# Storing scattered gate weights for 32 tokens at a time instead of 16, in a two-layer diffusion backbone step

## The chip, the cores and the metric

One core of one Trainium2 chip runs the whole program. The metric is device time in microseconds (us) of one execution; for several executions the median is given. A time of the kernel here is 3,980 us or so, so a tenth of a per cent is about 4 us.

## What is computed

Two trunk layers work on 128 context tokens and 512 latent tokens, 640 in all, 1024 features wide. Layer 0 mixes tokens by retention and a DFT, layer 1 by a convolution module. Each layer ends in the same channel mixer (PEER), and the change lies in that one alone:

```python
def peer(h, w_q, sub_keys, u_tab, v_tab):
    q = (x @ w_q).reshape(T, PEER_HEADS, 2, PEER_DQH)
    scores = jnp.einsum('thsd,hskd->thsk', q, sub_keys)
    s, i = lax.top_k(scores, PEER_TOPK)
    ...
    top, sel = lax.top_k(cand, PEER_TOPK)
    idx = jnp.take_along_axis(cidx, sel, axis=-1)
    g = jax.nn.softmax(top, axis=-1)
    ...
        a = jax.nn.gelu(jnp.einsum('td,thkd->thk', xb, u_tab[ib]))
        w = gb * a
        return jnp.einsum('thk,thkd->td', w, v_tab[ib])
```

Each token picks 8 x 16 = 128 of 16,384 experts. An expert is one row of `u_tab` and one row of `v_tab`; the token's output is the sum of its experts' v rows, each weighted by its gate `g` times the GELU of the token's product with the u row. All numbers are 32-bit floats.

## The kernel before

**Two ways through PEER.** Of the five blocks of 128 tokens, two (`GB = 2`) are done sparsely: GpSimd gathers each token's u and v rows by index (L711, 512 KB a gather), VectorE takes the products (`dot`, L1524) and adds the weighted v rows (`add`, L1559). The other three blocks (`DT` = 384 tokens) are done densely: TensorE multiplies with all 16,384 experts. For 32 of those tokens (`GQ`) the u side is done by gathers too (`qdot`, L1534).

**The dense way has two stages per layer.** In the *jobs* stage (`job`, L807) TensorE computes all u products of 352 tokens, 128 experts at a time, 128 such jobs (and 16 query projections), from weights that SyncE's queue loads into four slots (L591). ScalarE applies the GELU into `a_stage`, and SyncE stores it to DRAM (`acts`, L584) every fourth job. In the *values* stage (`values`, L876) TensorE walks over 32 chunks (`CHUNKS`) of 4 x 128 experts: for a chunk VectorE multiplies the activations read back (`acts`, L620) with the gates read back (L615) into `w_slot` (`weigh`, L1587 to L1601), and 48 matmuls (as the trace counts them) multiply `w_slot` with the chunk's v rows (`v_slot`, loaded at L607 and L623).

**The gates have to be scattered in between.** The dense way needs, for each token, the gates as a 128 x 128 table of experts with 128 entries filled. VectorE and ScalarE build one-hot rows for four tokens at a time (`OH = 4`: `hot`, L1562, L1571 and L1573; `build`, L1145), TensorE multiplies them into a PSUM bank (`scatter`, L844), and ScalarE copies the bank to a staging buffer (`take_scatter`, L1163). These 96 scatters per layer run amid the last two fifths of the jobs stage, placed by a planner's times (`peer_steps_of`, L486), with `LATE = 6`: all scatters stand before the last six jobs. This stretch is called the *scatter stretch* below.

**Staging, store and load.** There are two staging buffers (`g_stage`, L254). Each holds [128 first indices] x [128 second indices x `TQ` tokens]. After the fourth scatter into a buffer ScalarE's queue stores it to DRAM as one 1 MB piece (L1173), 24 a layer. A buffer is written again only after its store has landed (semaphores `g_out`, L1168). In the values stage SyncE loads the gates of two chunks at a time (1.5 MB, L615): 24 pieces per partition, each 8 second indices x 16 tokens x 4 bytes = 512 bytes.

**The queue of SyncE at the handover.** SyncE issues in program order. When the last u weights are issued, `peer_values` (L599) begins: the first chunk's v rows (2 MB, into `work[:, 5120:9216]`) wait for the scores (L603), done long before; then it waits until all scatters are copied and all stores landed (L609 to L611); then come the first gate load (L615), the second chunk's v rows, and the rest. VectorE's first `weigh` waits for that gate load, and TensorE's first values pass for that `weigh` (L888).

```python
1165  q, at = spot(b, g) // 4, g % 4
1167  if at == 0 and q >= 2:
1168      act.wait_ge(g_out[q % 2], l * G_OUT + 16 * (q // 2))
1171  if at == 3:
1172      act.wait_ge(sc_taken, l * len(sc_at[0]) + i + 1)
```

Of the kernel before, what the change touches and what calls it, by code (L numbers as in the profile page):

```python
# [32 lines left out]
NKEYS = 128  # L33
# [5 lines left out]
CT = 4  # L39
CHUNKS = NKEYS // CT  # L40
GCT = 8
TQ = 16
QS = DT // TQ
CE = CT * DT
GE = GCT * DT
# [1 line left out]
KEPT = 2  # L47
OH = 4
OHS = P // OH
HK = PHEADS * TOPK  # L50
GH = GB * PHEADS
ROWS = GH * TOPK
# [9 lines left out]
GQG = GQ // OH  # L62
BUILT = DB * OHS - GQG
LAG = 20
# [82 lines left out]
def program(nc, x_in, cond_t, norm_gain, final_gain, ada_w, ada_b, ada_fix_in, ab_w_in, ab_w_out, decays, states,  # L147
# [3 lines left out]
    with ctx:  # L151
# [10 lines left out]
        work = sb("work", [P, 15872])  # L162
# [88 lines left out]
        load_slot = [ring[:, i * 2048:(i + 1) * 2048] for i in range(4)]  # L251
        u_rows = [ring[:, 8192 + i * D:8192 + (i + 1) * D] for i in range(RING)]
        v_rows = [ring[:, 12288 + i * D:12288 + (i + 1) * D] for i in range(RING)]
        g_stage = [work[:, 10240 + i * 2048:12288 + i * 2048].rearrange("p (j t) -> p j t", j=NKEYS) for i in range(2)]  # L254
        a_stage = [work[:, 2048 + i * CA:2048 + (i + 1) * CA] for i in range(2)]
        hq = hT[:, :, 0:P]
        idx_q = q_t[:, 0:NQ].bitcast(U32)
# [97 lines left out]
        A_OUT, G_OUT, G_IN, A_IN = (16 * n for n in ((CHUNKS - KEPT) // 2, QS // 2, CHUNKS // 4, (CHUNKS - KEPT) // 2))  # L355
# [86 lines left out]
        def dve_order():  # L442
# [9 lines left out]
            picks += shared(NG - 1)  # L452
            hots = [("hot", b, g, 0, 1.45) for b in ORDER for g in range(OHS)]
            for m, hot in enumerate(hots):
# [31 lines left out]
        def peer_steps_of(jobs):  # L486

            ready, clock, begun, choosing = [], BEGIN, [0.0] * SCORE_LEAD, True
            for kind, a, b, i, w in dve_order():
# [18 lines left out]
                if kind == "hot":  # L508
                    ahead = ORDER.index(a) * OHS + b + OHB - 2
                    if ahead < DB * OHS and not 0 <= ahead - (DB - 1) * OHS < GQG:  # L510
                        ready.append((clock + 3, "build", ORDER[ahead // OHS], ahead % OHS))
# [31 lines left out]
        def spot(b, g):  # L543
            return ORDER.index(b) * OHS + g

# [23 lines left out]
        def _(sp):  # L569
# [29 lines left out]
            def peer_values(l):  # L599

                for n, c in enumerate(v_order):
                    if n == 0:
                        sp.wait_ge(scores, (l + 1) * BLOCKS * PHEADS)  # L603
                    elif n < 3:
                        sp.wait_ge(jobs_done, l * len(plans[0][1]) + len(plans[l][1]) - (2 - n) * CT)
                    if n < 3:
# [5 lines left out]
                    if n % 2 == 0:  # L612
                        if n >= 4:
                            sp.wait_ge(w_ready, l * CHUNKS + n - 2)
                        sp.dma_start(g_slot[n // 2 % 2].rearrange("p (q e) -> p q e", q=QS),  # L615
                                     gates_d[l].rearrange("q i e -> i q e")[:, :, c // 2 * GCT * TQ:(c // 2 + 1) * GCT * TQ]).then_inc(g_in[n // 2 % 2], 16)
                    if n >= KEPT:
# [444 lines left out]
        def _(act):  # L1062
# [49 lines left out]
            def peer(l):  # L1112
# [49 lines left out]

                def take_scatter(b, g):  # L1163
                    i = sc_at[l]["scatter", b, g]
                    q, at = spot(b, g) // 4, g % 4
                    act.wait_ge(sc_done, l * len(sc_at[0]) + i + 1)
                    if at == 0 and q >= 2:
                        act.wait_ge(g_out[q % 2], l * G_OUT + 16 * (q // 2))  # L1168
                    f(g_stage[q % 2][:, :, at * OH:(at + 1) * OH],
                      bank[:, 4 + i % SCB, :].rearrange("p (t j) -> p j t", t=OH)).then_inc(sc_taken, 1)  # L1170
                    if at == 3:
                        act.wait_ge(sc_taken, l * len(sc_at[0]) + i + 1)
                        nc.scalar.dma_start(gates_d[l, b * OHS // 4 + g // 4], g_stage[q % 2].rearrange("p j t -> p (j t)"))\  # L1173
                            .then_inc(g_out[q % 2], 16)

                for kind, a, i in steps:
# [27 lines left out]
            for i in range(len(items) + 1):  # L1204
                if i < len(items):
                    c, b = items[i]
# [8 lines left out]
                if 0 <= i - 1 < 4 * BLOCKS:  # L1215
                    c, b = items[i - 1]
# [41 lines left out]
            for i in range(PE_TILES):  # L1258
                t = KT - PE_TILES + i
# [4 lines left out]
            for i in range(PE_TILES):  # L1264
                t = KT - PE_TILES + i
# [27 lines left out]
        def _(v):  # L1293
# [101 lines left out]
            def peer(l):  # L1395
# [191 lines left out]
                def weigh(n):  # L1587
# [6 lines left out]
                    if n >= 3:  # L1594
                        v.wait_ge(v_done, l * (CHUNKS - 1) + n - 2)
                    skip = GQ // TQ
                    a = a_stage[n % 2].rearrange("p (j q t) -> p j q t", j=CT, q=QS - skip)
# [316 lines left out]
```

## Time and profile before

| what | value |
|---|---|
| median of 3 runs | 3982.68 us (3977.96 to 3985.86) |
| the profiled execution | 3988.73 us, span 3986.9 us |
| TensorE busy | 3840.1 us, 96% of the span |
| VectorE busy | 2642.8 us, 66% |
| ScalarE busy | 701.6 us, 18% |
| GpSimd busy | 1413.5 us, 35% |
| moved by DMA | 1155.58 MB, mean 290 GB/s |
| packets under 2 KB | 163,360 of 377,654 |

The profile is of one execution. "Busy" counts the instructions of an engine against the span; the four engines and the 16 DMA engines work side by side, so shares do not add up to 100%. The granted clock of TensorE is a share of full speed. An engine's idle time is put down to whatever ended it. A DMA is timed from its issue to its landing.

### The profile page before, as it was taken

To read this page: it belongs to the slowest core of one execution; us is meant where nothing else is said; L and a number is where in the kernel's file an instruction comes from. 1 tells how busy PE (TensorE), PEld (TensorE's weight loads), DVE (VectorE), ACT (ScalarE), POOL (GpSimd) and SP (SyncE) were. 2 spreads that over 40 slices of the span, in tenths; PEclk is the share of its full clock that TensorE was granted. 3 is DMA by queue.
4 is the path that set the end of the run, shared out by engine and by line. 5 is a ranking of instruction groups with operands and counts; after the bars stand their busy time and mean duration, and the time that the engine had idled before them with its cause. 6 is when DMAs were issued, how large, how long until landed. Compare 5 with 4: busy or idle time off the path is not lost.

```text
span 3986.9 us, 36490 instructions
## 1 busy us (share of the span) xinstructions
PE 3840.1 (96%) x12776; PEld 2195.3 (55%) x12776; DVE 2642.8 (66%) x5842; ACT 701.6 (18%) x1597; POOL 1413.5 (35%) x1180
## 2 busy tenths in 40 slices
PE   8999789999999999999998999999999999999998
PEld 1545556666666754444445545666666674444443
DVE  2681559998777845455535944999877884455554
ACT  1111011111345710000001221111134560000000
POOL 0110004555445434444420000455545543444341
PEclk9999989999999999999999999999999999999999
DMA  9452048999899999999972102899989999999994
GB/s 339 150 194 101 8 144 304 337 342 343 304 389 392 383 337 367 379 367 377 359 269 83 44 32 81 320 338 329 350 305 406 386 370 338 368 368 381 366 370 172
DMA packets 377654, 1155.58 MB, mean 290 GB/s; under 512 B 28720, under 2 KB 163360, under 8 KB 346360
## 3 DMA queue, kind: packets, MB, share of 16 engines
q0 software_dynamic: 170016, 618.96, 42.2%
q1 hardware_dynamic: 198368, 483.93, 33.0%
q10 hardware_dynamic: 9088, 50.37, 3.1%
q8 instruction: 102, 1.67, 0.2%
q14 instruction: 80, 0.66, 0.0%
HBM read 1055.68 MB, written 97.40 MB: 289 GB/s over the span
## 4 chain that ended last, share of the span: by engine, by line
PE 84%; DVE 7%; DMA 7%; ACT 1%; issue 1%; POOL 1%; ACTq 0%; DVEq 0%; SPq 0%
PE bank L759 83%; DMA ring<-in_peer_u,q_t 3%; DMA ring<-in_peer_v,work 2%; DVE ring L1693 1%; DMA ring<-in_peer_u,work 1%; DVE diag L1559 1%; DVE ring L1534 1%; DVE bc L1573 1%; DMA ring<-in_ada_w 1%; POOL ring L711 1%; DVE ring L1524 1%; DVE bc L1571 0%; DMA peer_gates<-work 0%; ACT work L1065 0%; ACT hT L1065 0%
## 5 line engine op out<-in xcount | busy, mean ns | idle before, releaser
L759 PE MATMUL bank<-hT,ring 128*128 128x352 f32 (+3 forms) x5696 | 1682.7, 454 | 3.3 <-ACT hT L1065 3.3
L759 PEld LDWEIGHTS bank<-hT,ring 128*128 128x128 f32 x5696 | 1054.0, 192 | 556.7 <-issue 75.2
L711 POOL DMA_INDIRECT ring<-in_peer_u,work x512 | 730.3, 1426 | 1339.5 <-DVE ring L1524 1042.3
L759 PE MATMUL bank<-ring,work 128*128 128x512 f32 x2016 | 868.8, 592 | 0.0
L1559 DVE SCALAR_TENSOR_TENSOR diag<-ring,work,diag 128x1024 f32<-128x1024 f32 x508 | 652.9, 1285 | 110.0 <-DMA ring<-in_peer_v,work 99.9
L1524 DVE SCALAR_TENSOR_TENSOR ring<-ring,work 128x1024 f32<-128x1024 f32 x512 | 624.4, 1220 | 99.8 <-DMA ring<-in_peer_u,work 99.6
L711 POOL DMA_INDIRECT ring<-in_peer_v,work x512 | 555.2, 1084 | 284.6 <-issue 148.5
L759 PEld LDWEIGHTS bank<-ring,work 128*128 128x128 f32 x2016 | 383.0, 190 | 482.2 <-issue 482.2
L1065 ACT ACTIVATE work<-bank 128x352 f32<-128x352 f32 (+3 forms) x528 | 272.3, 524 | 1465.8 <-PE bank L759 1414.0
L759 PE MATMUL bank<-work 128*128 128x512 f32 x1056 | 457.0, 592 | 1.1 <-ACT work L1065 1.1
L759 PE MATMUL bank<-ring,hT 128*128 128x384 f32 (+1 forms) x960 | 353.4, 525 | 8.5 <-ACT hT L1065 8.5
L759 PEld LDWEIGHTS bank<-work 128*128 128x128 f32 x1056 | 200.5, 190 | 253.8 <-issue 251.6
L1600 DVE COPY work<-bc 128x128 f32<-128x128 f32 x64 | 14.3, 224 | 487.7 <-DMA work<-peer_acts 427.3
L759 PEld LDWEIGHTS bank<-ring,hT 128*128 128x128 f32 x960 | 180.3, 191 | 172.1 <-issue 84.7
L759 PE MATMUL bank<-bc 128*128 128x128 f32 x1536 | 197.9, 281 | 38.4 <-DVE bc L1573 27.6
L759 PEld LDWEIGHTS bank<-bc 128*128 128x128 f32 x1536 | 190.7, 195 | 65.6 <-DVE bc L1573 40.0
L1065 ACT ACTIVATE work<-work 128x16 f32<-128x16 f32 (+3 forms) x49 | 14.2, 304 | 1124.8 <-DVE ring L1524 1112.9
L1571 DVE TENSOR_SCALAR bc<-keep,small 128x128 f32<-128x128 f32 x416 | 123.4, 343 | 55.6 <-PE bank L759 45.4
L1065 ACT ACTIVATE bc<-work,small 128x128 f32<-128x128 f32 x352 | 152.7, 483 | 0.0
L1830 DVE SCALAR_TENSOR_TENSOR work<-work,small 128x670 f32<-128x670 f32 x180 | 149.4, 908 | 0.0
L1573 DVE TENSOR_TENSOR bc<-small,keep 128x512 f32<-128x512 f32 x192 | 130.8, 681 | 0.0
L1065 ACT ACTIVATE work<-keep,small 128x128 f32<-128x128 f32 x352 | 120.8, 393 | 30.8 <-PE bank L759 14.2
(178 smaller groups left out, 2060.9 us busy)
## 6 DMA issues: line engine op xcount, KB each, us to landing
ring<-in_peer_ut SPq DMA_DIRECT2D x128, 1024.0 KB, 8.6
ring<-in_peer_vt SPq DMA_DIRECT2D x42, 2048.0 KB, 11.3
peer_gates<-work ACTq DMA_DIRECT2D x48, 1024.0 KB, 8.6
bc<-peer_gates SPq DMA_DIRECT2D x32, 1536.0 KB, 31.1
work<-in_peer_vt SPq DMA_DIRECT2D x22, 2048.0 KB, 11.3
peer_acts<-work SPq DMA_DIRECT2D x60, 704.0 KB, 6.1
work<-peer_acts SPq DMA_DIRECT2D x60, 704.0 KB, 14.6
ring<-in_ada_w SPq DMA_DIRECT2D x12, 2048.0 KB, 14.4
```

The lines of the kernel that those rows point to most:

```text
L711: nc.gpsimd.indirect_dma_start(row, None, table, bass.IndirectOffsetOnAxis(ap=at, axis=0)).then_inc(s, 16)
L759: return nc.tensor.matmul(out, lhsT, rhs, start=start, stop=stop, **kw)
L1065: return nc.scalar.activation(out, in_, func, **kw)
L1524: v.scalar_tensor_tensor(out=row, in0=row, scalar=1.0, in1=h_tok[:, n % GB, :], op0=ALU.mult, op1=ALU.mult, accum_out=dots[:, n % 2, k:k + ...
L1534: v.scalar_tensor_tensor(out=row, in0=row, scalar=1.0, in1=hq, op0=ALU.mult, op1=ALU.mult, accum_out=dots_q[:, i:i + 1]).then_inc(u_free, 1)
L1559: v.scalar_tensor_tensor(out=a, in0=row, scalar=wgt[:, n % 2, k:k + 1], in1=a, op0=ALU.mult, op1=ALU.add).then_inc(v_free, 1)
L1571: v.tensor_scalar(oh[:, n % OHB, 0, o, :], iota, ijg_t[:, b, 0, t0 + o:t0 + o + 1], ijg_t[:, b, 2, t0 + o:t0 + o + 1], ALU.is_equal, ALU.mult)
L1573: v.tensor_tensor(oh[:, n % OHB, 1, :, :], ijg_t[:, b, 1, t0:t0 + OH].unsqueeze(2).to_broadcast([P, OH, NKEYS]), iota.unsqueeze(1).to_broa ...
L1600: v.tensor_copy(w[:, :, 0:skip, :], g[:, :, 0:skip, :])
L1693: ins = v.scalar_tensor_tensor(out=a, in0=w, scalar=by, in1=a, op0=ALU.mult, op1=ALU.add)
L1830: ins = v.scalar_tensor_tensor(out=y_conv[:, f, :], in0=src, scalar=w, in1=y_conv[:, f, :], op0=ALU.mult, op1=ALU.add)
```

## The change

`TQ`, the tokens that a staging buffer holds, goes from 16 to 32, and a buffer and its store from 1 MB to 2 MB. There are 12 stores per layer in place of 24, each after the eighth scatter (`TG = TQ // OH = 8`). The DRAM layout follows, so a gate load reads 12 pieces of 1 KB per partition in place of 24 of 512 bytes. The two buffers together now take `work[:, 6144:14336]` in place of `work[:, 10240:14336]`, which reaches into the place of the first chunk's v rows (`work[:, 5120:9216]`); so the load of these rows gets a wait for the stores of buffer 0. In `weigh` the views follow from `TQ` (`skip` is 1 in place of 2, and the inner runs are 32 elements long).

```diff
-TQ = 16
+TQ = 32
...
+TG = TQ // OH
...
-        g_stage = [work[:, 10240 + i * 2048:12288 + i * 2048].rearrange("p (j t) -> p j t", j=NKEYS) for i in range(2)]
+        g_stage = [work[:, 6144 + i * 4096:10240 + i * 4096].rearrange("p (j t) -> p j t", j=NKEYS) for i in range(2)]
...
                     if n == 0:
                         sp.wait_ge(scores, (l + 1) * BLOCKS * PHEADS)
+                        sp.wait_ge(g_out[0], (l + 1) * G_OUT)
...
-                    q, at = spot(b, g) // 4, g % 4
+                    q, at = spot(b, g) // TG, g % TG
                     act.wait_ge(sc_done, l * len(sc_at[0]) + i + 1)
                     if at == 0 and q >= 2:
                         act.wait_ge(g_out[q % 2], l * G_OUT + 16 * (q // 2))
...
-                    if at == 3:
+                    if at == TG - 1:
                         act.wait_ge(sc_taken, l * len(sc_at[0]) + i + 1)
-                        nc.scalar.dma_start(gates_d[l, b * OHS // 4 + g // 4], g_stage[q % 2].rearrange("p j t -> p (j t)"))\
+                        nc.scalar.dma_start(gates_d[l, b * OHS // TG + g // TG], g_stage[q % 2].rearrange("p j t -> p (j t)"))\
                             .then_inc(g_out[q % 2], 16)
```

How the instructions stand. First SyncE's queue at the handover of layer 0 (`in_peer_vt` are v rows, `peer_gates` the gates, `peer_acts` the activations), before:

```order
L591 DMA ring<-in_peer_ut 128x2048
L607 DMA work<-in_peer_vt 128x4096 [waits scores]
L615 DMA bc<-peer_gates 128x24x128 [waits g_out1,g_out0,sc_taken]
L607 DMA ring<-in_peer_vt 128x4096 [waits jobs_done] x2
L615 DMA bc<-peer_gates 128x24x128
```

and with the change (lines are 1 or 2 higher):

```order
L592 DMA ring<-in_peer_ut 128x2048
L609 DMA work<-in_peer_vt 128x4096 [waits g_out0,scores]
L617 DMA bc<-peer_gates 128x12x256 [waits g_out1,g_out0,sc_taken]
L609 DMA ring<-in_peer_vt 128x4096 [waits jobs_done] x2
L617 DMA bc<-peer_gates 128x12x256
```

The order of the queue is the same; the first v rows have moved behind the last store of buffer 0 by their wait, and the gate load has half the pieces.

Second, ScalarE at the last scatters of layer 0 (`work<-bank 128x128x4` is the copy of a scatter, `128x352` that of a job), before:

```order
L1065 ACTIVATE work<-bank 128x128x4 [waits sc_done]
L1173 DMA peer_gates<-work 128x2048 [waits sc_taken]
L1065 ACTIVATE work<-keep,small 128x128 [waits sc_done,oh_built]
L1065 ACTIVATE work<-keep,small 128x128
L1065 ACTIVATE bc<-work,small 128x128 [waits far_ready] x2
L1065 ACTIVATE work<-bank 128x128x4 [waits g_out0,sc_done]
...
L1065 ACTIVATE work<-bank 128x128x4 [waits g_out1,sc_done]
L1065 ACTIVATE work<-bank 128x128x4 [waits sc_done] x3
L1173 DMA peer_gates<-work 128x2048 [waits sc_taken]
L1065 ACTIVATE work<-bank 128x352 [waits jobs_done] x2
```

and with the change:

```order
L1067 ACTIVATE work<-bank 128x128x4 [waits sc_done]
L1175 DMA peer_gates<-work 128x4096 [waits sc_taken]
L1067 ACTIVATE work<-keep,small 128x128 [waits sc_done,oh_built]
L1067 ACTIVATE work<-keep,small 128x128
L1067 ACTIVATE bc<-work,small 128x128 [waits far_ready] x2
L1067 ACTIVATE work<-bank 128x128x4 [waits g_out1,sc_done]
...
L1067 ACTIVATE work<-bank 128x128x4 [waits sc_done] x4
L1175 DMA peer_gates<-work 128x4096 [waits sc_taken]
L1067 ACTIVATE work<-bank 128x352 [waits jobs_done] x2
```

The last store stands at the same place, behind the last scatter's copy, and is twice as large; of the three stores ahead of it only the middle one is left. TensorE, VectorE and GpSimd have the same instructions in the same order as before.

## Rows read from the trace of the kernel before

**Rows 1.** The page: TensorE's busy time; the chain that ended last, by engine.
```profile
PE 3840.1 (96%) x12776; PEld 2195.3 (55%) x12776; DVE 2642.8 (66%) x5842; ACT 701.6 (18%) x1597; POOL 1413.5 (35%) x1180
...
PE 84%; DVE 7%; DMA 7%; ACT 1%; issue 1%; POOL 1%; ACTq 0%; DVEq 0%; SPq 0%
```

**Rows 2.** Busy time by stretch: scatter stretch, values of layer 0; scatter stretch of layer 1.
```profile
core 0: us, PE busy (x) PEld busy (x) DVE busy (x) ACT busy (x) POOL busy (x), PEclk, DMA share, GB/s
1060.00:1434.00 374.00, 353.75 (x1655) 255.96 (x1654) 280.38 (x540) 201.56 (x516) 172.43 (x138) 0.99 0.96 373
1434.00:2093.00 659.00, 659.00 (x1536) 291.61 (x1536) 339.65 (x409) 6.11 (x15) 277.39 (x227) 1.00 0.95 351
2939.00:3314.00 375.00, 354.94 (x1652) 256.74 (x1650) 280.41 (x538) 200.82 (x516) 175.52 (x138) 0.99 0.96 372
```

**Rows 3.** SyncE's queue at the handover of layer 0, in order of time.
```profile
1369.34 1.25 SPq L607 DMA_DIRECT2D work<-in_peer_vt  x1
1413.41 0.38 SPq L615 DMA_DIRECT2D bc<-peer_gates  x1
1414.39 19.26 SPq L607 DMA_DIRECT2D ring<-in_peer_vt  x2
```

**Rows 4.** ScalarE's queue, layer 0: the last stores of gates, in order of time.
```profile
1391.98 0.33 ACTq L1173 DMA_DIRECT2D peer_gates<-work  x1
...
1404.74 0.33 ACTq L1173 DMA_DIRECT2D peer_gates<-work  x1
```

**Rows 5.** VectorE and TensorE at the handover of layer 0, in order of time.
```profile
1403.87 29.43 PE L759 MATMUL bank<-hT,ring 128*128 128x352 f32 x96
...
1427.68 0.23 DVE L1600 COPY work<-bc 128x128 f32<-128x128 f32 x1 [15.56 <-DMA bc<-peer_gates]
1427.83 1.62 DVE L1601 TENSOR_TENSOR work<-work,bc 128x1408 f32<-128x1408 f32 x1
...
1433.85 20.87 PE L759 MATMUL bank<-work 128*128 128x512 f32 x48 [0.55 <-ACT work L1065]
```

**Rows 6.** The chain of waits at the end of layer 1's jobs: start, us, what.
```profile
3282.60 31.24 PE bank L759 x104
3314.38 638.88 PE bank L759 x1488
```

**Rows 7.** VectorE's first weigh in layer 1, in order of time.
```profile
3308.45 1.62 DVE L1601 TENSOR_TENSOR work<-work,bc 128x1408 f32<-128x1408 f32 x1
```

**Rows 8.** DMA issues from 1369 to 1372 us: KB each, us to landing.
```profile
work<-in_peer_vt SPq DMA_DIRECT2D x1, 2048.0 KB, 17.1
peer_gates<-work ACTq DMA_DIRECT2D x1, 1024.0 KB, 13.3
```

**Rows 9.** The page: DMA issues of the whole run, median us to landing.
```profile
ring<-in_peer_vt SPq DMA_DIRECT2D x42, 2048.0 KB, 11.3
peer_gates<-work ACTq DMA_DIRECT2D x48, 1024.0 KB, 8.6
bc<-peer_gates SPq DMA_DIRECT2D x32, 1536.0 KB, 31.1
```

**Rows 10.** Busy time by stretch around the handover of layer 0 (columns as in rows 2).
```profile
1392.00:1400.00 8.00, 4.63 (x35) 3.98 (x35) 7.96 (x18) 7.45 (x20) 3.41 (x4) 1.00 0.97 372
...
1413.40:1420.00 6.60, 6.60 (x24) 4.27 (x23) 0.00 (x0) 0.93 (x2) 1.73 (x2) 1.00 1.04 408
1420.00:1427.70 7.70, 7.70 (x27) 4.95 (x27) 0.01 (x1) 0.46 (x1) 0.00 (x0) 1.00 1.15 347
```

**Rows 11.** ScalarE in layer 1's scatter stretch: the one long wait for a store.
```profile
3149.31 0.34 ACTq L1173 DMA_DIRECT2D peer_gates<-work  x1
...
3166.51 0.60 ACT L1065 ACTIVATE work<-bank 128x512 f32<-128x512 f32 x1 [6.26 <-DMA peer_gates<-work]
```

**Rows 12.** What TensorE waited for, 2939 to 3180 us: us in total, times, longest.
```profile
PE bank L759 <- ACT work L1065: 2.4, 1, 2.4
```

**Rows 13.** Busy time between layers 0 and 1 (columns as in rows 2).
```profile
2111.00:2120.00 9.00, 7.59 (x28) 6.15 (x29) 0.92 (x5) 3.17 (x3) 0.00 (x0) 0.56 0.01 2
```

## The prediction

> **What bounds the kernel now.** I read the page first: TensorE is busy for 3840.1 us, 96% of the span, and 84% of the chain that ended last is TensorE's [rows 1]. So only what moves TensorE's idle time, some 147 us in all, can move the end. The busy times by stretch say where the change could touch it [rows 2]. In the values stage of layer 0 TensorE is busy for 659.00 of 659.00 us: there is nothing to gain, though the 16 DMA engines are at 0.95. In the two scatter stretches it idles for 374 - 353.75 = 20.2 us and 375 - 354.94 = 20.1 us, with the DMA engines at 0.96. Between the two stages lies the handover, and there the change puts its wait.
>
> The handover is a chain: last scatter copied, store landed, gate load landed, first `weigh`, first values pass. In layer 0 the last store is issued at 1404.74 [rows 4] and the gate load at 1413.41 [rows 3], 8.67 us later; VectorE starts at 1427.68, 14.27 us after that, ended by the gate load, and finishes at 1427.83 + 1.62 = 1429.45 [rows 5]. TensorE is still at its last jobs, for 29.43 us from 1403.87, and starts the values at 1433.85 [rows 5]. So the chain has 1433.85 - 1429.45 = 4.4 us to spare. In layer 1 it is the same: `weigh` ends at 3308.45 + 1.62 = 3310.07 [rows 7], the values start at 3314.38 [rows 6], 4.3 us to spare.
>
> **The change, part by part.**
>
> *Fewer stores.* 24 of 48 stores go, with 0.33 us each on ScalarE's queue [rows 4], 8 us in all. ScalarE is not the bound: where it is fullest, just before the handover, it is busy for 7.45 of 8 us, but VectorE for 7.96 of 8 [rows 10], and the scatters wait for both. I cost this at nothing; VectorE is the cover.
>
> *A buffer that lasts twice as long.* A buffer is reused after eight scatters of the other one instead of four, and its store is twice as large. In layer 1 one store took from 3149.31 to 3166.5, and ScalarE waited 6.26 us for it [rows 11], TensorE 2.4 us for ScalarE [rows 12]. With the change the scatter that waited there fills the second half of a buffer and waits for nothing. I take -2.4 us; the bounds are 0 (another store is late instead) and -6.3 (all that ScalarE waited).
>
> *The v rows moved.* The first 2 MB of v rows leave the scatter stretch, where they were issued at 1369.34 [rows 3], and wait for the last store of buffer 0. That one now stands at 1391.98 [rows 4] and should land at about 1407, so the rows should land by 1407 + 17.1 [rows 8] = 1424, with 9 us to spare before TensorE wants them. Queued behind the new wait on SyncE are the gate load and the later v rows; the gate load waits for the other buffer's store anyway, and the second chunk's v rows are wanted 20.87 us [rows 5] after the first. So the wait itself costs nothing. But the rows now travel beside the last store.
>
> *The last store, twice as large.* This is the term that matters: it is on the chain, twice per run. From below: a 2 MB load of v rows lands in 11.3 us in the median of the run [rows 9]. From above: the 1 MB store that travelled beside the first v rows took 13.3 us [rows 8], twice that is 26.6. Nearest are the v rows of that same moment, 2 MB beside a store and the gathers, at 17.1 us [rows 8]; since the u weights that were also under way then are done by the last store, I take 16. The chain grows by 16 - 8.67 = 7.3 us.
>
> *The gate load in pieces of 1 KB.* It moves the same 1.5 MB with half the pieces. While it lands, the core's DMA moves 408 GB/s at first and 347 at the end, with shares above 1 [rows 10]. Had it kept 408, the 408 x 6.6 + 347 x 7.7 = 5.36 MB would have taken 13.1 us instead of 14.3. I take -1.2 us for that; the bounds are 0 and half the load, -7.1.
>
> The Trainium skill speaks against this term: its page "DMA: Bandwidth & Descriptors" (section Specifications) puts the smallest transfer for line rate at 512 bytes, which the old pieces already have. By that the load keeps its 14.27 us, and the sum below would be 2.4 us higher. The trace half agrees, since the rate beside the old pieces is 347 to 408 GB/s [rows 10], no less than the 351 of the values stage [rows 2].
>
> Later gate loads are hidden: they land in 31.1 us [rows 9], one for each two chunks, which TensorE needs 2 x 20.87 = 41.7 us for [rows 5].
>
> *The strides.* `weigh` takes runs of 32 elements instead of 16, 1.62 us for 1408 elements [rows 5]. A gain there is hidden: VectorE is busy for 339.65 of 659 us of the values stage [rows 2].
>
> **The sum.** Per layer the chain grows by 7.3 - 1.2 = 6.1 us, of which 4.4 are spare: TensorE starts the values 1.7 us later, 3.5 us for both layers. Minus 2.4 in layer 1's scatter stretch: +1.1 us. The pause of TensorE before the values grows from 0.55 to 2.3 us. Between the layers, after a longer pause, its granted clock was 0.56 for 9 us [rows 13], so a longer pause might cost up to 4 us more in each layer; for so short a one I take nothing. Against the profiled execution's 3988.73 us that is 3989.8. That execution lies 6.05 us above the median of the three runs, 3982.68; against the median it is **3984 us**: no change that can be told. What a measurement of this kernel can tell is some 0.2%, 8 us.
>
> **The rivals.**
>
> *Slower: the last store takes the place of the spare time.* If store, v rows and gathers share the DMA engines evenly and the store takes 26.6 us, the chain grows by 17.9 us, and TensorE stands still for 13.5 us at each handover: +27 - 2.4 = +25 us, 4007. For it: the DMA engines are at 0.96 in that stretch [rows 2], and 3 MB more than before travel between the last scatter and the gate load. Against it: the v rows took only 17.1 us in the same crowd [rows 8]. It decides from a store of about 19.5 us on: there each handover costs 5.2 us, and the sum passes 8. Chance 0.17.
>
> *Slower: the gate load gets slower, not faster.* The pieces of one partition now lie 2 MB apart in DRAM instead of 1 MB, and the partitions 16 KB instead of 8 KB. If that costs a quarter, 14.27 becomes 17.8, the 1.2 are lost too, and each handover costs 4.8 us more: 1.1 + 9.6 = +11, 3993. The values stage would still hide it, 31.1 x 1.25 = 39 against 41.7. No row speaks for it or against it. Chance 0.05.
>
> The Trainium skill's page "DMA: Bandwidth & Descriptors" (section Latency and other measured facts) tells of such a loss for partitions spaced by large powers of two, 207 GB/s at 512 KB and 164 at 2 MB; here that distance lies between pieces, not partitions, so the chance is small.
>
> *Faster: the scatter stretches close up.* If the freed 2 MB, the rarer stores and the rarer waits took away half of TensorE's 20.2 + 20.1 us of idle time there [rows 2], it would be -20 us, 3963. For it: the DMA engines are nearly full there. Against it: the gates' bytes are the same, 2 MB at 373 GB/s [rows 2] are 5.6 us of 374, and they leave at the end, where VectorE and not DMA is full [rows 10]. Chance 0.10.
>
> **How the numbers follow.** The forecast, everything within 0.2% of before, has what is left, 0.68. Its own range is 3976 to 3991. The range of 8 in 10 reaches down to part of the faster case, 3972, and up to a store of 24 us, which costs 9.7 us at each handover and +17 in sum, 4000. Faster by over 0.2%: 0.10. Slower: 0.17 + 0.05 = 0.22. Within: 0.68.
>
> **What the profile of the changed kernel would show.** Right: 24 stores of 2 MB; the last one of a layer landing 14 to 19 us after its issue; the gate load issued near 1421 and landing in about 13 us; TensorE's values starting 1 to 4 us after its last job; the values stage gapless as before; and no wait of ScalarE for a store in layer 1. Wrong: a pause before the values of 6 us or more, or none at all with a store under 13 us; a total that moved by more than 8 us with the handover as forecast would mean that the scatter stretch changed, and its idle time would show it.

## The result, and the profile after

The changed kernel takes 4000.45 us (median of 5, 3992.72 to 4003.7) where the kernel before, timed beside it, takes 3982.68 (median of 5). The ratio is 1.0045 [1.0032, 1.0057]: 18 us slower, more than the 8 us that a measurement can tell. The forecast was no change, 3984 us, and its range ended at 4000.

The profiled executions are 3998.75 us after (span 3996.9) and 3988.73 before (span 3986.9), 10.0 us apart. The one before lies 6.0 us above its median and the one after 1.7 below, so the two traces hold only 10 of the 18 us (more on this at the end of the section). Their spans divide at events that can be seen in both: the first and last 352-column jobs around the scatters, and the first values matmul.

| stretch | before | after | difference |
|---|---|---|---|
| scatter stretch, layer 0 | 335.6 | 339.6 | +4.0 |
| last six jobs to first values pass, layer 0 | 30.0 | 32.8 | +2.8 |
| values of layer 0 and up to layer 1's jobs | 1019.2 | 1022.5 | +3.3 |
| scatter stretch, layer 1 | 337.5 | 335.8 | -1.7 |
| last six jobs to first values pass, layer 1 | 30.2 | 32.1 | +1.9 |
| values of layer 1 and the end | 672.5 | 675.5 | +3.0 |
| all else | | | -3.3 |

The last line is nearly all layer 0's start, before the first changed instruction: the scatter stretch begins at 1068.1 us before and at 1065.0 after, and between 1063.5 and 1073.4 in the profiles of all runs below.

The page of the kernel after has the line of busy time, the chain's shares, and the DMA issues (KB each, median us to landing):

```profile
PE 3848.2 (96%) x12776; PEld 2203.1 (55%) x12776; DVE 2638.6 (66%) x5842; ACT 699.4 (17%) x1597; POOL 1403.0 (35%) x1180
...
PE 83%; DMA 8%; DVE 7%; issue 1%; ACT 1%; POOL 1%; DVEq 0%; SPq 0%
...
ring<-in_peer_vt SPq DMA_DIRECT2D x42, 2048.0 KB, 12.0
peer_gates<-work ACTq DMA_DIRECT2D x24, 2048.0 KB, 12.0
```

TensorE does the same 12,776 matmuls in 8.1 us more [rows 1]: it is not only idle longer, it is also slower. Half as many stores, twice the size, land in 12.0 us where one of 1 MB took 8.6 [rows 9].

**The handover.** SyncE's and ScalarE's queues after, layer 0, in order of time (start, us):

```profile
1405.58 0.33 ACTq L1175 DMA_DIRECT2D peer_gates<-work  x1
```

```profile
1401.72 0.33 SPq L609 DMA_DIRECT2D work<-in_peer_vt  x1
1419.94 0.38 SPq L617 DMA_DIRECT2D bc<-peer_gates  x1
```

The gate load follows the last store by 14.36 us in place of 8.67 [rows 3, 4]. The first v rows, which left at 1369.34 before [rows 3], now leave 4 us ahead of that store and travel beside it. They land 15.2 us later, 3 us before the gate load leaves. What they and the store hold up are the gathers: those issued from 1400 to 1413 us land in 17 us (DMA issues of that time, KB each where the size is known, median us to landing),

```profile
work<-in_peer_vt SPq DMA_DIRECT2D x1, 2048.0 KB, 15.2
...
ring<-in_peer_u,work POOLq DMA_INDIRECT x4, 17.1
```

where the kernel before, from 1399 to 1412 us, has

```profile
ring<-in_peer_u,work POOLq DMA_INDIRECT x4, 8.9
```

So nine late gathers still travel beside the gate load, up to 1433.2; before there were eight, up to 1423.3. The chain that ended last now runs through both transfers, in layer 0 and in layer 1 (start, us, what):

```profile
1405.58 14.29 DMA peer_gates<-work
...
1419.94 15.39 DMA bc<-peer_gates
...
3290.22 13.29 DMA peer_gates<-work
...
3303.58 15.75 DMA bc<-peer_gates
```

In the profile before, this chain went through TensorE's jobs [rows 6]. VectorE and TensorE after, in order of time:

```profile
1404.71 29.09 PE L761 MATMUL bank<-hT,ring 128*128 128x352 f32 x96
1437.47 8.71 PE L761 MATMUL bank<-work 128*128 128x512 f32 x13 [3.67 <-DVE work L1603]
```

```profile
1435.42 0.23 DVE L1602 COPY work<-bc 128x128 f32<-128x128 f32 x1 [13.45 <-DMA bc<-peer_gates]
```

TensorE waits 3.67 us for `weigh` where it waited 0.55 for ScalarE [rows 5]. And then it is slow. Busy time by stretch after, around its restart in layer 0 and in layer 1:

```profile
core 0: us, PE busy (x) PEld busy (x) DVE busy (x) ACT busy (x) POOL busy (x), PEclk, DMA share, GB/s
1437.40:1442.00 4.60, 4.53 (x6) 1.98 (x7) 1.46 (x1) 0.00 (x0) 0.00 (x0) 0.50 0.98 415
1442.00:1447.00 5.00, 5.00 (x12) 2.19 (x11) 0.00 (x0) 0.00 (x0) 0.00 (x0) 0.87 1.06 353
...
3321.40:3327.00 5.60, 5.56 (x7) 2.50 (x8) 1.45 (x1) 0.00 (x0) 0.00 (x0) 0.50 0.99 423
```

and the first of these stretches in the kernel before, where the values already run:

```profile
1437.40:1442.00 4.60, 4.60 (x12) 2.08 (x11) 0.00 (x0) 0.00 (x0) 0.00 (x0) 1.00 1.02 374
```

Six matmuls in place of twelve: the granted clock is 0.50, the 1.2 GHz level, for some 5 us after the pause. The whole values stages in the chain show the price, 2.9 us more in layer 0 (the row of before stands in the second fence) and 3.0 more than the 638.88 of layer 1 before [rows 6]:

```profile
1437.47 662.35 PE bank L761 x1536
...
3321.44 641.84 PE bank L761 x1488
```

```profile
1433.85 659.48 PE bank L759 x1536
```

**The scatter stretch.** The three windows of [rows 2], after:

```profile
1060.00:1434.00 374.00, 354.89 (x1643) 258.24 (x1641) 275.93 (x529) 198.06 (x513) 175.18 (x138) 0.97 0.95 366
1434.00:2093.00 659.00, 655.53 (x1521) 290.67 (x1522) 337.51 (x409) 4.23 (x13) 269.18 (x227) 0.99 0.93 353
2939.00:3314.00 375.00, 358.55 (x1663) 260.89 (x1662) 278.11 (x536) 201.86 (x517) 176.47 (x141) 0.98 0.95 367
```

The values stage is no longer gapless because it starts 3.5 us into its window. In the stretches TensorE looks a little busier, but at a granted clock of 0.97 and 0.98 in place of 0.99, and in layer 0 with 12 matmuls fewer. A window that lies wholly inside the stretch shows more: the same 207 us of layer 0's stretch, before and after:

```profile
1066.00:1273.00 207.00, 196.08 (x860) 137.96 (x859) 149.88 (x271) 95.88 (x246) 99.55 (x85) 0.99 0.95 370
```

```profile
1066.00:1273.00 207.00, 195.56 (x843) 138.17 (x842) 148.46 (x269) 94.67 (x244) 102.24 (x83) 0.97 0.93 356
```

After, the DMA engines move less, 356 GB/s in place of 370, and TensorE gets through 843 matmuls in place of 860. What VectorE waited for in that window, before (us in total, times, longest):

```profile
DVE ring L1534 <- DMA ring<-in_peer_u,q_t: 20.3, 13, 3.4
DVE diag L1559 <- DMA ring<-in_peer_v,work: 12.5, 8, 3.1
DVE ring L1524 <- DMA ring<-in_peer_u,work: 11.7, 8, 5.2
```

and after:

```profile
DVE ring L1526 <- DMA ring<-in_peer_u,work: 19.9, 5, 8.6
DVE diag L1561 <- DMA ring<-in_peer_v,work: 16.4, 7, 7.1
DVE ring L1536 <- DMA ring<-in_peer_u,q_t: 12.4, 7, 5.7
```

It waits for gathered rows 19 times in place of 29, and each time longer: the longest are 5.7 to 8.6 us in place of 3.1 to 5.2. The landing times of the gathers say how (all gathers of that window, us; before, after):

```profile
DMA to landing us min/median/max: 4.7/10.3/15.8
```

```profile
DMA to landing us min/median/max: 4.7/9.0/18.6
```

Half of the gathers land sooner than before, and the slowest land later. VectorE takes them in order, so it waits for the late ones.

So two things are suspected: the last store's size beside the moved v rows at the handover, and the size of every store beside the gathers in the stretch. The table shows little of the second, 673.1 us for both stretches before and 675.4 after. But the profiled execution of before lies 6 us above its median; the run below that changes only the last store, so that its stretch is the one of before, took 667 us there in an execution 2.5 us below its median.

### The profile page after: what moved, and what is told of

It is laid out like the page before. It is cut to its first block, busy times and chain, and to the rows that moved or that the text cites. A ratio compares the mean times of both kernels' runs of the same rounds, so it can differ in the third digit from the quotient of the medians.

```text
span 3996.9 us, 36444 instructions
## 1 busy us (share of the span) xinstructions
PE 3848.2 (96%) x12776; PEld 2203.1 (55%) x12776; DVE 2638.6 (66%) x5842; ACT 699.4 (17%) x1597; POOL 1403.0 (35%) x1180
## 4 chain that ended last, share of the span: by engine, by line
PE 83%; DMA 8%; DVE 7%; issue 1%; ACT 1%; POOL 1%; DVEq 0%; SPq 0%
PE bank L761 83%; DMA ring<-in_peer_u,q_t 3%; DMA ring<-in_peer_v,work 2%; DVE ring L1695 1%; DMA bc<-peer_gates 1%; POOL ring L713 1%; DMA peer_gates<-work 1%; DVE diag L1561 1%; DMA ring<-in_peer_u,work 1%; DVE ring L1536 1%; DMA ring<-in_ada_w 1%; DVE bc L1575 1%; DVE bc L1573 0%; DVE ring L1526 0%; ACT hT L1067 0%
## 5 line engine op out<-in xcount | busy, mean ns | idle before, releaser
L713 POOL DMA_INDIRECT ring<-in_peer_v,work x512 | 538.6, 1052 | 326.6 <-DVE diag L1561 184.8
## 6 DMA issues: line engine op xcount, KB each, us to landing
bc<-peer_gates SPq DMA_DIRECT2D x32, 1536.0 KB, 28.3
```

The source lines that it names most:

```text
L713: nc.gpsimd.indirect_dma_start(row, None, table, bass.IndirectOffsetOnAxis(ap=at, axis=0)).then_inc(s, 16)
```

## The experiments

Each was timed against the kernel before on the same chip; a ratio has its 95% interval. "Both stretches" is the sum of the two scatter stretches of the profiled execution, measured as in the table: before 673.1, after 675.4.

### A pause without the slow clock

Five idle matmuls, whose results are never read, follow the last job.

```diff
                 pe.wait_ge(sc_taken, l * len(sc_at[0]) + len(sc_at[l]))
+                for n in range(5):
+                    mm(bank[:, 6, 0:DU], ident, hT[:, n, T0 + GQ:T], True, True)
```

> The changed kernel, with five idle matmuls (128x352, 0.6 us each, result never read) between TensorE's last job and its first values pass, so that TensorE does not stand still while it waits for the first weigh. Handover theory (TensorE stands for 3.7 us at each handover and then runs at half clock for 5 to 8 us): the values start no earlier than in the changed kernel, but the granted clock stays near 1.00 and the values stage takes 659.5 us in layer 0 instead of 662.4; 2.9 us saved per layer, about 4000.5 - 6 = 3994.5. Scatter theory (the loss lies in the scatter stretch, from 2 MB bursts that hold up the gathers): no change, 4000.

Measured: 3995.78, ratio 1.0043 [1.003, 1.0055]. TensorE's timeline and its clock at the handover:

```profile
1434.38 3.23 PE L761 MATMUL bank<-hT,keep 128*128 128x352 f32 x10 [0.55 <-ACT work L1069]
1437.44 13.04 PE L761 MATMUL bank<-work 128*128 128x512 f32 x30
```

```profile
1437.40:1442.00 4.60, 4.60 (x12) 2.09 (x11) 0.68 (x1) 0.00 (x0) 0.00 (x0) 1.00 1.00 423
```

The values start at the same time, 1437.44, and the clock is 1.00: twelve matmuls again. The chain has the idle matmuls (ten, as the trace counts them) and the values stage in one piece:

```profile
1434.38 662.44 PE bank L761 x1546
```

From 1437.44 on these are 659.4 us, in place of 662.35. So the slow clock comes from the pause. In the median this did not show: the ratio is that of the change within the interval, and both stretches took 680.8 us here. On the time the run is inconclusive.

### The wait and the doubled store, each alone and together

The first edit puts only the moved v rows into the kernel before:

```diff
                         sp.wait_ge(scores, (l + 1) * BLOCKS * PHEADS)
+                        sp.wait_ge(g_out[0], (l + 1) * G_OUT)
```

The second only doubles the last store: a second 1 MB goes out behind it, to a block that nobody reads, and the gate load waits for it too.

```diff
                             .then_inc(g_out[q % 2], 16)
+                        if q == QS - 1:
+                            nc.scalar.dma_start(gates_d[l, QS], g_stage[0].rearrange("p j t -> p (j t)")).then_inc(g_out[1], 16)
...
-                            sp.wait_ge(g_out[i], (l + 1) * G_OUT)
+                            sp.wait_ge(g_out[i], (l + 1) * (G_OUT + 16 * i))
```

The third is both.

> The kernel before with one line added: the first v rows wait for the last store of buffer 0, as in the change; stores of 1 MB, pieces of 512 bytes. Handover theory: the last store now travels beside 2 MB of v rows and lands after about 13.3 us instead of 8.67, as the store did that was beside them before; the chain grows by 4.6 us of which 4.4 are spare, so TensorE stands for 0 to 1 us more: 3982 to 3986. Scatter theory: the scatter stretch is 2 MB lighter, so it is the same or a few us faster, 3977 to 3983.

> The kernel before, with a second 1 MB store (the other buffer once more, to a place nobody reads) right behind the last one of each layer, for which the first gate load also waits: the last store is doubled alone, with the v rows early. Handover theory: gate load issued 11 to 13 us after the last store instead of 8.67, within the 4.4 us that are spare: 3982 to 3986. Scatter theory: the stretch is as before, 3982.7.

> The kernel before with both: the first v rows wait for buffer 0, and the last store is doubled. Scatter stretch and pieces of 512 bytes as before. Handover theory: the chain of the changed kernel; gate load issued 14 us after the last store, TensorE stands for 3 to 4 us and restarts at half clock for 2.9 us more: 5 to 7 us per layer, 3993 to 3997, that is most of the measured 17.8 us. Scatter theory: the 1 MB stores leave the stretch as it was, so at most 3986.

Measured: the wait alone 1.002 [1.0011, 1.0029], the store alone 1.0001 [0.9993, 1.001], both 1.004 [1.0027, 1.0053]. The chains at layer 0's handover, wait alone:

```profile
1399.67 12.80 DMA peer_gates<-work
1412.55 15.73 DMA bc<-peer_gates
```

store alone, with its values stage:

```profile
1399.22 13.44 DMA peer_gates<-work
1412.73 13.12 DMA bc<-peer_gates
...
1427.96 659.45 PE bank L759 x1536
```

and both:

```profile
1400.87 17.94 DMA peer_gates<-work
...
1434.11 661.41 PE bank L760 x1536
```

A doubled store by itself lands in 13.4 us, and the 4.4 us to spare nearly cover it: TensorE pauses 1.36 us (1.97 in layer 1), and the values keep their 659.45 us. Beside the v rows even the 1 MB store takes 12.80 us and the gate load 15.73, so the pause is 2.98 us; in layer 1 the store takes 9.2, the gate load, which there leaves 4.5 us before the v rows are in, 19.4, and the pause is 2.96. With both, the store takes 17.94 and the pause is 5.86 us. From the last store's issue to VectorE's start on the gates it is 22.9 us before, 26.7 with the doubled store, 28.7 with the moved v rows, 31.2 with both and 29.8 in the changed kernel (layer 0). So the moved v rows weigh more than the doubled store, and among these kernels only those with them have a pause above 2 us. The wait alone was expected to cost 1 us or less at each handover and missed by that.

In both kernels with the wait the two scatter stretches of the profile are shorter, 662.3 and 663.9 us: the v rows are gone from them. The times don't show this as a gain, as the next kernels tell.

### Undoing the meeting

The first v rows are issued right behind the first gate load, in the kernel before and in the changed one:

```diff
-                    if n < 3:
+                    if 0 < n < 3:
                         sp.dma_start(v_slot[n].rearrange("p j d -> p (j d)"), peer_vt[l, c]).then_inc(v_in[n], 16)
...
                             .then_inc(g_in[n // 2 % 2], 16)
+                    if n == 0:
+                        sp.dma_start(v_slot[n].rearrange("p j d -> p (j d)"), peer_vt[l, c]).then_inc(v_in[n], 16)
```

> The kernel before with one statement moved: the first v rows are issued right behind the first gate load instead of 40 us ahead of it. If the v rows of 2 MB in the scatter stretch cost that stretch what the runs with the wait suggest (330 to 333 us instead of 333 to 337) and the rows, issued 20 us ahead of the first values pass, land in time, then the scatter stretches gain 2 to 4 us per layer and the handover loses nothing: ratio 0.998 to 0.999. If the v rows land late (over 20 us) TensorE waits for them: ratio 1.001 to 1.003.

> The changed kernel with the same statement moved: the first v rows behind the first gate load, so that the last 2 MB store travels without them. Handover theory: the store lands after about 11 us instead of 14, weigh comes 3 us earlier, TensorE stands for 1 us or less and keeps its clock: 4 to 5 us per layer, ratio 1.002 instead of 1.0045. If the first v rows are then late instead, the same pause with another cause: 1.004 to 1.005.

Measured: the kernel before with it 1.0007 [0.9998, 1.0015], the changed one 1.0032 [1.0018, 1.0045]. The changed kernel's first values pass, layer 0:

```profile
1440.97 9.28 PE L763 MATMUL bank<-work 128*128 128x512 f32 x21 [0.55 <-ACT work L1069]
```

The pause is back at 0.55 us (0.73 in layer 1), and 13 of the 18 us are still there. Both scatter stretches take 676.2 us in the changed kernel and 662.0 in the one before, with the same v rows out of the way. So a second cost lies in the stretch. The kernel before was expected to gain 0.1 to 0.2% from this move and gained nothing: its profile lies 5 us below its median as that of before lies 6 above, and TensorE now waits 1.59 and 1.04 us for the late v rows. That the v rows cost the stretch of the kernel before something is therefore not shown.

### The stretch: the rows of a store, or its bytes at once

With 32 tokens a store has 16 KB per partition in place of 8. Two kernels cut the changed kernel's store into four pieces of 4 KB, or two of 8 KB per partition, all sent at once. A third is the kernel before with the wait, four buffers of 16 tokens, and two 1 MB stores sent together after each eighth scatter.

```diff
+                        for c in range(4):
+                            at = slice(c * NKEYS * TQ // 4, (c + 1) * NKEYS * TQ // 4)
+                            nc.scalar.dma_start(gates_d[l, b * OHS // TG + g // TG][:, at], g_stage[q % 2].rearrange("p j t -> p (j t)")[:, at])\
+                                .then_inc(g_out[q % 2], 16)
```

```diff
-                    if at == 3:
+                    if at == 3 and q % 2:
                         act.wait_ge(sc_taken, l * len(sc_at[0]) + i + 1)
+                        for c in (q - 1, q):
...
```

> The changed kernel with each 2 MB store issued as four stores of 512 KB, one behind the other, so that its rows are 4 KB long, like the gathers' rows, instead of 16 KB. The two profiles with 2 MB stores show scatter stretches of 336 to 341 us per layer, against 330 to 333 in the two kernels with 1 MB stores and late v rows. Row theory (long rows take a larger share of a DMA engine's turns and hold up the gathers): the stretch falls to about 332 us, ratio to before 1.000 to 1.003 instead of 1.0045. Burst theory (2 MB at once, in rows of whatever length): no change, 1.004 to 1.005. A last store with a smaller share could land later and take some of a gain back at the handover.

> The kernel before (16 tokens, 1 MB stores, 8 KB rows, gate pieces of 512 bytes) with four staging buffers in the place that the change uses, stored two at a time: 2 MB at once after every eighth scatter, as in the change, and the v rows waiting as in the change. Burst theory: scatter stretch 336 to 341 us per layer, ratio 1.005 to 1.008. Row theory: 330 to 334 us as with single 1 MB stores, ratio 1.004, that of the run with the doubled last store and the wait, whose handover this has.

> The changed kernel with each 2 MB store issued as two stores of 1 MB with rows of 8 KB, the row length of before; layout, bytes and moment of issue as in the changed kernel. Row theory: scatter stretches of 330 to 334 us per layer in the profile, as with the paired stores of 8 KB rows (334.1 and 329.6), and 3 to 10 us less in the median than the changed kernel: ratio 1.002 to 1.004. Burst theory: 336 to 341 us and 1.0045.

> The kernel with the paired 1 MB stores once more, for a second profile, since its median (1.0055) and its one profile (the fastest of its runs) told two stories. Row theory: scatter stretches near 334 and 330 us again and the loss at the handover, 33 to 34 us. Burst theory: 336 to 341 us in this profile.

> The changed kernel itself once more, beside the others on one chip, for a second profile. Both theories: ratio 1.0045 within its interval, handover 32 to 33 us in each layer from the first of the last six jobs to the first values pass (30.0 and 30.2 before). Row and burst theory: scatter stretches of 336 to 341 us. If they came out at 330 to 334, the difference between profiles would be chance and neither theory would hold.

| run | ratio | both stretches |
|---|---|---|
| four pieces of 4 KB | 1.0038 [1.0024, 1.0052] | 668.4 |
| two pieces of 8 KB | 1.005 [1.0034, 1.0066] | 676.9 |
| before, 1 MB stores in pairs | 1.0055 [1.004, 1.007] | 663.7 |
| the same again | 1.0042 [1.0026, 1.0057] | 676.8 |
| the changed kernel again | 1.0056 [1.0043, 1.0068] | 677.6 |

The first profile of the pairs, 663.7 us, is of the fastest of its executions, 3988.65 us where the median is 3995.55. In the second run the stretches took 676.8. Rows of 8 KB cost as much as rows of 16 KB, and the staging, layout and gate loads of the kernel before cost as much as the new ones, as soon as 2 MB leave at once. The theory of the long rows fell. This rests on the profiles: in the time the pairs can't be told from the kernel above with the wait and the doubled last store (1.004), whose stretch has 1 MB stores. The four pieces of 4 KB lie between in the profile, and in the time can't be told from the changed kernel; that stays open.

The same 207 us, in the kernel before with pairs:

```profile
1066.00:1273.00 207.00, 193.24 (x832) 136.53 (x831) 146.49 (x267) 95.01 (x244) 99.69 (x85) 0.97 0.92 356
```

### Spreading the bytes, alone and with late v rows

The changed kernel's buffers and layout, but each 2 MB store goes in two halves, the second four scatters later (the last one at once). The second kernel also issues the first v rows behind the gate load.

```diff
                     if at == TG - 1:
                         act.wait_ge(sc_taken, l * len(sc_at[0]) + i + 1)
+                        store_half(q, 0)
+                        if q == QS - 1:
+                            store_half(q, 1)
+                    if at == TG // 2 - 1 and q:
+                        store_half(q - 1, 1)
```

> The changed kernel with each 2 MB store in two halves, the first after the eighth scatter, the second four scatters later (the last store of a layer still at once): 1 MB at a time, as before, with the changed buffers and layout. Burst theory: scatter stretches of 330 to 334 us per layer instead of 336 to 341, the handover as in the changed kernel (32 to 33 us), 8 to 13 us off the median: ratio 1.002 to 1.003. If the larger buffers or the layout were the cause: 336 to 341 us and 1.0045 to 1.0055.

> The same, and the first v rows behind the first gate load, which took the pause out of the changed kernel's handover (30.8 and 31.0 us). Both causes undone: scatter stretches of 330 to 334 us, handover 30 to 31 us, ratio 0.998 to 1.001, so nothing of the loss is left, with pieces of 1 KB all the same. If a third cause is hidden in the change, 1.002 or more is left.

Measured: 1.0024 [1.001, 1.0038], and with late v rows 0.9999 [0.999, 1.0008]. Both stretches take 661.7 and 663.8 us. The 207 us of the first:

```profile
1066.00:1273.00 207.00, 199.97 (x876) 141.08 (x875) 151.29 (x276) 97.37 (x249) 99.20 (x85) 0.99 0.94 371
```

and VectorE's longest wait for gathers there:

```profile
DVE ring L1535 <- DMA ring<-in_peer_u,work: 15.3, 8, 5.5
```

371 GB/s again, 876 matmuls, and 5.5 us in place of 8.6. The gathers of the window are as even as before:

```profile
DMA to landing us min/median/max: 4.8/10.1/15.2
```

In all eight profiles with 2 MB at once the median is 8.9 to 9.6 and the slowest 17.2 to 19.0 us; in all nine with 1 MB at a time, the kernel before among them, they are 9.8 to 10.4 and 14.2 to 15.8. The last kernel's first values pass, layers 0 and 1:

```profile
1429.30 20.84 PE L763 MATMUL bank<-work 128*128 128x512 f32 x48 [0.92 <-DMA work<-in_peer_vt]
```

```profile
3305.34 4.94 PE L763 MATMUL bank<-work 128*128 128x512 f32 x7 [3.04 <-DMA work<-in_peer_vt]
```

In layer 1 the late v rows cost a pause of their own, 3.04 us. Even so, with both undone the changed kernel is level with the one before, so whatever else is in the change costs nothing that can be told, and the pieces of 1 KB, which are still there, gain nothing. The two causes show in the time one by one: late v rows with the burst and without it are 1.0032 [1.0018, 1.0045] and 0.9999 [0.999, 1.0008], spreading with the v rows beside the last store and without them 1.0024 [1.001, 1.0038] and 0.9999. Of the 18 us, late v rows alone gave back 5, spreading alone 8, both together 18; that the two don't add is within the intervals, some 5 us each, and which of them is the larger the runs don't tell.

### Keeping only the part that helped

The v rows out of the scatter stretch, but not beside the last store: the kernel before, its first v rows waiting until all but ten scatters are copied; and the same with `LATE = 5`.

```diff
+                        sp.wait_ge(sc_taken, l * len(sc_at[0]) + len(sc_at[l]) - 10)
```

> The kernel before with one line added: the first v rows wait until all but ten scatters are copied, some 18 us ahead of the last store, where VectorE and not DMA is full. If the 2 MB cost the scatter stretch its 2 to 4 us per layer only where DMA is full, and if the rows are through before the last store: scatter stretches of 330 to 333 us and a handover of 30 us, ratio 0.998 to 0.999, the fastest of all. If they still travel beside the last store: as the run with the wait alone, 1.001 to 1.002.

> The kernel before with the v rows in mid-stretch, as in the run that was level with before (0.9994), and five jobs instead of six behind the last scatter, to use the spare 4.4 us of the handover. Handover from the first of the five jobs to the first values pass 25.5 to 26.5 us instead of 29.3, the scatter stretch 4.7 us longer by the job less what TensorE idled there: 1 to 3 us less per layer, ratio 0.997 to 0.999. If the job delays the last scatters in full, or the pause drops the clock: 0.999 to 1.002.

Measured: 0.9994 [0.9985, 1.0003] and 1.0013 [1.0004, 1.0022]. Both stretches take 664.6 us in the first, but the time can't be told from before. The second fell on the worse of its two forecasts and is a little slower than before: the gates were not read back any sooner, so the job that was taken away came back as a pause of 4.9 us at each handover, with the slow clock behind it. No version beat the kernel before.

## Why the prediction was wrong, point by point

- **The last store, twice as large.** Taken as 16 us to the gate load; it was 14.36 in layer 0 and 13.4 in layer 1. The place was right, and the size a little high. The v rows beside it were reckoned to leave at about 1407; they left at 1401.72, since the last store of buffer 0 landed in 9.5 us and not in 15.
- **The gate load in pieces of 1 KB.** Taken as 1.2 us faster; it was 1.2 slower, 15.48 us from issue to VectorE against 14.27. The term looked at the load's own pieces and took what travels beside it as given. The v rows were in 3 us before the load left, but the gathers that they and the store had held up were not: nine gathers ran beside it in place of eight. Over all handovers the load's landing goes with that number: 10.0 and 10.4 us with four and five gathers (four pieces of 4 KB), 15.2 to 17.3 with nine or ten; where the v rows were still under way too (the wait alone) it was 15.7 and 19.4. That this is the cause is read from the traces and was not tested by itself. The pieces show no clear effect here: with eight gathers the old ones landed in 14.2 to 16.3 us, the new ones in 13.4 to 15.1. By the Trainium skill's page "DMA: Bandwidth & Descriptors" (section Specifications), 512 bytes already reach line rate. The handover agrees; but over the whole run the median gate load landed in 28.3 us in place of 31.1 (27.9 to 28.8 in the eight profiles with pieces of 1 KB, 30.8 to 32.4 in the nine with 512 bytes), a tenth sooner, where it is hidden. The rates that the prediction held beside this rule, 347 to 408, are not all "no less than the 351".
- **The pause.** Forecast as 2.3 us; it was 3.67 us in layer 0 and 3.48 in layer 1. The values started 2.8 and 1.9 us later, where 1.7 and 1.8 were forecast: the sum of the two terms above, with the sign of the second turned.
- **The clock.** "A longer pause might cost up to 4 us more in each layer; for so short a one I take nothing": this term was mis-sized. It measured 2.9 and 3.0 us in the two layers, nearly as much as the pause itself, and 1.7 in each when the changed kernel ran again. Over both layers of all runs, pauses of 0.55 to 1.97 us left the values stage at its length, 659.5 us in layer 0; those of 2.57 to 5.90 made it 1.5 to 3.0 us longer, the long ones no more than the short ones.
- **A buffer that lasts twice as long, and fewer stores.** With the clock, this is the step that failed. The two were put at -2.4 us and nothing; the scatter stretches got some 8 to 13 us slower. The wait of 6.26 us [rows 11] did go: ScalarE's list of waits in layer 1's stretch names no store any more. But the step looked only at the buffer's owner. The same edit sends 2 MB at once into a stretch whose DMA engines are at 0.96 [rows 2], and the prediction's "Fewer stores" priced only the 0.33 us of issue. That is where the rest of the time went: both stretches took 675 to 681 us in six of the eight profiles with 2 MB at once (663.7 in the first one of the pairs, 668.4 with four pieces), and 662 to 665 with 1 MB at a time and the v rows out of the stretch.
- **The v rows moved.** "The wait itself costs nothing" did not hold: put alone into the kernel before it cost 1.002 [1.0011, 1.0029], 8 us, with a pause of 3 us at each handover. The prediction saw that the rows would travel beside the last store and put this into the store's size, not into the gate load. Taking 2 MB out of the stretch may have gained something there, 662 to 665 us in the profiles for both stretches where the kernel before took 673 and, with only the doubled store, 667; but the kernel before with late v rows was no faster, so the gain is not shown in the time.
- **The rivals.** The slower one had the right place, the last store at the expense of the spare time, and the wrong lever: it needed a store of 19.5 us to pass 8 us in all, and with one of 14 the handovers and the clock made 10.6. The strided pieces cost nothing: with them and both causes undone the kernel is level with before. The faster one had the stretch right and its sign wrong.
- **The last line of the prediction** said that a total off by over 8 us with the handover as forecast would point to the scatter stretch. The values started 4.7 us later in sum [2.8 + 1.9 of the table], where 3.5 were forecast, and the clock added 5.9. That is 10.6 of the 18 us, so the sentence held: the rest is the stretch, by the runs that undid one of the two causes 8 to 13 us, each within some 5.

The measured time lies half a microsecond above the range, but that is no near miss: the forecast's sum left out the burst and the clock, and put the gate load the wrong way.

What is argued and not shown is why 2 MB at once delay some gathers more than 1 MB twice. Fewer and longer waits, and gathers that are faster in the median and slower at the worst, suggest that the gathers in flight ride over a short store and not over a long one. By the Trainium skill's page "DMA: Bandwidth & Descriptors" (section Queues, rings and completion order) each DMA engine takes turns between its queues packet by packet. By that rule a store only shares the way, and one would expect the same bytes to cost the gathers the same in all. The rates here differ, 353 to 363 GB/s with 2 MB at once and 368 to 374 with 1 MB in the same 207 us (367 for four pieces); no run here separates the engines' turns from the order in which VectorE takes the gathers.

## What to carry to other kernels

Where the DMA engines are nearly full, batch size is a matter of what else is in flight: halving the number of transfers saved issue time that nobody waited for, and the burst delayed the loads that somebody did. When an edit moves a transfer, list what it then travels beside, and price those as well as the transfer itself. When a chain's spare time runs out, price the restart on the slow clock too: here pauses of TensorE of 2.6 to 5.9 us cost 1.5 to 3 us beyond their length. And before a difference between two profiles is read as an effect, look where each profiled execution lies among its own kernel's times.

## What the runs showed of the hardware

A pause of 3.5 to 3.7 us after some 29 us of unbroken matmuls brought the granted clock to 0.50 for some 5 us; in all runs, pauses of 2.57 to 5.90 us cost 1.5 to 3.0 us beyond themselves and those up to 1.97 us nothing; idle matmuls in the pause kept the clock at 1.00. A second 1 MB sent right behind the first landed with it in 13.4 us, and beside 2 MB of v rows in 17.9. With 2 MB stores in place of 1 MB ones among the gathers, the same bytes, the median gather of the 207 us landed in 9.0 us in place of 10.3 and the slowest in 18.6 in place of 15.8. One profile can mislead: of two profiled executions of the same kernel, the scatter stretches differed by 13 us.
